# Reordering the delta-rule stage of a two-block layer: convolution taps in halves, squares, norms and the last pair's gate at other places of the queues

## The reference, cut to what matters

```python
def _gdn_mixer(h, w_in, conv_w, a_log, dt_bias, o_gain, w_out):
    ...
    proj = h @ w_in
    qkv = jax.nn.silu(_causal_conv(proj[..., :3 * W], conv_w)).astype(jnp.float32)
    z = proj[..., 3 * W:4 * W]
    ...
    q = _l2norm(qkv[..., :W]) * (Dh ** -0.5)
    k = _l2norm(qkv[..., W:2 * W])
    beta = jax.nn.sigmoid(b_raw)
    g = -jnp.exp(a_log) * jax.nn.softplus(a_raw + dt_bias)
    o = _chunk_gated_delta(q, k, v, g, beta)
    o = _rms(o, o_gain) * jax.nn.silu(z)
    return o @ w_out
```

## Time and profile before

| what | value |
|---|---|
| median of 3 runs | 900.2 us (900.01 to 903.18) |
| the profiled execution, its own time | 899.58 us |
| its span, first to last instruction | 897.8 us |
| TensorE / VectorE / ScalarE busy | 811.9 / 639.2 / 497.8 us |
| mean granted TensorE clock | 0.975 |
| stage of the delta rule, in the span | about 478 to 709 us |

### The profile page before, as it was taken

How to read it: one execution, slowest core, us unless ns; L and a number is a source line. 1 busy time by engine, 2 the same in 40 slices (tenths; PEclk the granted TensorE clock), 3 DMA queues, 4 the chain that set the end, 5 groups by cost and what they waited for, 6 DMA issues and landing times.

```text
span 897.8 us, 16865 instructions
## 1 busy us (share of the span) xinstructions
PE 811.9 (90%) x7056; PEld 752.0 (84%) x7056; DVE 639.2 (71%) x1284; ACT 497.8 (55%) x1013; POOL 0.2 (0%) x4
## 2 busy tenths in 40 slices
PE   4988999999999999999978788989888879999988
PEld 3877999989999999999967586868777869978888
DVE  4467977896687888978868677676655577955464
ACT  4566744444556666654555635454662356666862
POOL 0000000000000000000000000000000000000000
PEclk9999999999999999999999899999997999999999
DMA  8522764765455566548762422121224236754211
GB/s 342 208 91 91 260 231 168 281 235 204 172 189 188 206 210 232 201 145 284 267 240 81 153 66 79 58 86 57 87 95 141 95 128 230 284 203 142 94 48 48
DMA packets 22684, 148.50 MB, mean 165 GB/s; under 512 B 2640, under 2 KB 3024, under 8 KB 6480
## 3 DMA queue, kind: packets, MB, share of 16 engines
q1 hardware_dynamic: 22608, 147.43, 46.3%
HBM read 146.37 MB, written 1.05 MB: 164 GB/s over the span
## 4 chain that ended last, share of the span: by engine, by line
PE 66%; DVE 21%; ACT 11%; issue 2%; DMA 1%; SPq 0%; DVEq 0%; ACTq 0%
PE ps L1960 51%; DVE wlo L1467 4%; DVE raw L1488 2%; DVE tmp L1464 1%; DVE qT L1464 1%; DVE vt L1464 1%; DVE kT L1464 1%; ACT L1050 1%; ACT whi L1071 1%; PE pp L2137 1%; PE pp L2114 1%; PE pp L2299 1%; DVE p0lo L1467 1%; PE pp L2178 1%; PE pp L2310 1%
## 5 line engine op out<-in xcount | busy, mean ns | idle before, releaser
L1960 PE MATMUL ps<-p0hi,whi 128*128 128x256 f32 x1128 | 333.0, 295 | 20.8 <-DVE p0lo L1467 13.6
L1960 PE MATMUL ps<-p0lo,whi 128*128 128x256 f32 x1128 | 320.2, 284 | 0.0
L1960 PE MATMUL ps<-p0hi,wlo 128*128 128x256 f32 x1128 | 319.4, 283 | 0.0
L1467 DVE TENSOR_TENSOR wlo<-raw,whi 128x512 fp32r<-128x512 f32 (+2 forms) x436 | 274.3, 660 | 22.3 <-ACT whi L1071 21.9
L1960 PEld LDWEIGHTS ps<-p0hi,whi 128*128 128x128 f32 x1128 | 217.1, 192 | 33.5 <-issue 15.7
L1071 ACT ACTIVATE whi<-raw 128x512 fp32r<-128x512 f32 (+2 forms) x436 | 238.6, 599 | 2.7 <-DMA raw<-wst 2.7
L1960 PEld LDWEIGHTS ps<-p0lo,whi 128*128 128x128 f32 x1128 | 217.4, 193 | 0.9 <-issue 0.7
L1960 PEld LDWEIGHTS ps<-p0hi,wlo 128*128 128x128 f32 x1128 | 217.1, 192 | 0.0
L1488 DVE CUSTOM_DVE_ANT_0 raw<-raw,cact,vc 128x1024 f32<-128x1024 f32 x64 | 81.8, 1278 | 0.0
L1960 PE MATMUL ps<-zhi,whi 128*128 128x256 f32 x176 | 49.8, 283 | 0.9 <-DVE wlo L1467 0.9
L1960 PE MATMUL ps<-zlo,whi 128*128 128x256 f32 x176 | 49.1, 279 | 0.0
(11 more groups left out here) (344 smaller groups left out, 1357.8 us busy)
## 6 DMA issues: line engine op xcount, KB each, us to landing
raw<-wst SPq DMA_DIRECT2D x125, 1024.0 KB, 4.9
raw<-wsd SPq DMA_DIRECT2D x16, 704.0 KB, 4.0
x<-xT SPq DMA_DIRECT2D x4, 256.0 KB, 5.1
m_x<-memT SPq DMA_DIRECT2D x1, 1024.0 KB, 8.6
outT<-x SPq DMA_DIRECT2D x4, 256.0 KB, 2.4
cact<-cB SPq DMA_DIRECT2D x1, 512.0 KB, 13.7
cst<-con SPq DMA_DIRECT2D x1, 356.0 KB, 12.0
smo<-conr SPq DMA_DIRECT2D x1, 320.0 KB, 11.7
```

What stands on the lines that cost most here:

```text
L1467: return v.tensor_tensor(lo, src, hi.bitcast(F32), ALU.subtract)
L1960: ins = t.matmul(o, a, b, start=first and q == 0, stop=last and q == len(ops) - 1, skip_group_check=True)
```

## The change

In the list: the taps of a unit are put off in two halves, one to each of the next two steps (half 0, one tile, then half 1, the other tile), and the SiLUs go with the second. The gate's transpose `g_tp` goes one round behind its copy `g_cp`; `g_ctp` and `g_col` come one round sooner, `g_exp` and `g_c3` stay in their round. `d_ones` comes one round behind `d_sq`, where two stood between, and `d_nrm`, `d_vtp`, `d_vb` one round behind `d_rs`. `d_on` comes a round behind `d_ors`. For pair 3 alone, `d_oz` reads the PSUM bank and multiplies by gain and gate, and `d_on` then multiplies by the norm; `d_ohi` and `d_olo` follow at a round's distance each. In the engines' code, only the taps' loop, `d_on`, `d_oz` and the names waited for differ; the number of instructions is the same.

```diff
 def on_mqk(i):
     def rest():
-        add("ctap", i)
+        add("ctap", i, 1)
         ...
-    later(rest)
+    self.deferred.extend([lambda: add("ctap", i, 0), rest])
 def on_qkva(u):
     def rest():
-        add("gtap", u)
+        add("gtap", u, 1)
         if u >= 8:
             add("gsilu", u - 8)
-    later(rest)
+    self.deferred.extend([lambda: add("gtap", u, 0), rest])
 def gdn_gates():
     ...
     add("g_cp", 2)
+    yield
     add("g_tp", 2)
-    yield
     add("g_abs", 2)
     ...
     add("g_m", 2)
-    for _ in range(4):
+    for _ in range(3):
         yield
     add("g_ctp", 2)
     add("g_col", 2)
+    yield
     add("g_exp")
     add("g_c3")
 def gdn(i):
     ...
     yield
-    yield
     for n in range(2):
         add("d_ones", i, n)
         add("d_rs", i, n)
+    yield
+    for n in range(2):
         add("d_nrm", i, n)
     ...
     add("d_oones", i)
     add("d_ors", i)
+    if i == 3:
+        add("d_oz", i)
+        add("d_on", i)
+        yield
+        add("d_ohi", i)
+        yield
+        add("d_olo", i)
+        return
+    yield
     add("d_on", i)
 def frees(name, i):
+    if name in ("mqk", "qkva"):
+        return on(FREES[name], i, 1)
 # VectorE, d_on
+    if n_ == 3:
+        e.wait_ge(*on("d_oz", n_))
+        v.tensor_tensor(qv, qv, tr[3 * (n_ % 2)], ALU.mult).then_inc(*tick("d_on"))
 # VectorE, d_oz
+    if n_ == 3:
+        e.wait_ge(*on("d_osq", n_))
+        stt(qv, ps[3 + 2 * (n_ % 2)], V("o_gain"), zv, ALU.mult, ALU.mult).then_inc(*tick("d_oz"))
```

More of the change, by code:

```diff
@@ L1156, in _ @@
                     v = flat(mqk[:, 2 * n:2 * n + 2, :])
-                    e.wait_ge(*on("ctap", n))
+                    e.wait_ge(*on("ctap", n, 1))
                     silu(v, v).then_inc(*tick("csilu"))
@@ L1221, in _ @@
                     n, = i
-                    e.wait_ge(*on("gtap", n + 8))
+                    e.wait_ge(*on("gtap", n + 8, 1))
                     for v in (qT, kT):
@@ L1416, in _ @@
                     n_, = i
-                    e.wait_ge(*on("d_oz", n_))
+                    e.wait_ge(*on("d_on" if n_ == 3 else "d_oz", n_))
                     e.wait_ge(*unit_done("za", 3))
@@ L1578, in _ @@
                 elif kind in ("ctap", "gtap"):
-                    n, = i
+                    n, m = i
                     if kind == "ctap":
@@ L1586, in _ @@
                         e.wait_ge(*on("gid", n))
-                    for m in range(2):
-                        for s in range(1, 4):
-                            if s > 1:
-                                e.wait_ge(*own.last)
-                            o = dst[:, m * T + s:(m + 1) * T]
-                            ins = stt(o, bank[:, m * T:(m + 1) * T - s], V(wname, (2 * n + m) * 4 + 3 - s), o, ALU.mult, ALU.add)
-                            if m * s == 3:
-                                ins.then_inc(*tick(kind))
-                            else:
-                                own.mark(ins)
+                    for s in range(1, 4):
+                        if s > 1:
+                            e.wait_ge(*own.last)
+                        o = dst[:, m * T + s:(m + 1) * T]
+                        ins = stt(o, bank[:, m * T:(m + 1) * T - s], V(wname, (2 * n + m) * 4 + 3 - s), o, ALU.mult, ALU.add)
+                        if s == 3:
+                            ins.then_inc(*tick(kind))
+                        else:
+                            own.mark(ins)
                 elif kind == "mv":
@@ L1884, in _ @@
                     n_, = i
+                    qv = flat(qT[:, 2 * n_:2 * n_ + 2, :])
                     e.wait_ge(*on("d_ors", n_))
-                    stt(flat(qT[:, 2 * n_:2 * n_ + 2, :]), ps[3 + 2 * (n_ % 2)], V("o_gain"), tr[3 * (n_ % 2)], ALU.mult, ALU.mult).then_inc(*tick("d_on"))
+                    if n_ == 3:
+                        e.wait_ge(*on("d_oz", n_))
+                        v.tensor_tensor(qv, qv, tr[3 * (n_ % 2)], ALU.mult).then_inc(*tick("d_on"))
+                    else:
+                        stt(qv, ps[3 + 2 * (n_ % 2)], V("o_gain"), tr[3 * (n_ % 2)], ALU.mult, ALU.mult).then_inc(*tick("d_on"))
                 elif kind == "d_oz":
@@ L1889, in _ @@
                     qv = flat(qT[:, 2 * n_:2 * n_ + 2, :])
-                    e.wait_ge(*on("d_on", n_))
+                    zv = flat(sz[:, 2 * n_:2 * n_ + 2, :])
                     e.wait_ge(*on("za", n_))
-                    v.tensor_tensor(qv, qv, flat(sz[:, 2 * n_:2 * n_ + 2, :]), ALU.mult).then_inc(*tick("d_oz"))
+                    if n_ == 3:
+                        e.wait_ge(*on("d_osq", n_))
+                        stt(qv, ps[3 + 2 * (n_ % 2)], V("o_gain"), zv, ALU.mult, ALU.mult).then_inc(*tick("d_oz"))
+                    else:
+                        e.wait_ge(*on("d_on", n_))
+                        v.tensor_tensor(qv, qv, zv, ALU.mult).then_inc(*tick("d_oz"))
                 elif kind == "d_olo":
```

## The result

The changed kernel took 887.1 us (median of 4 runs, 884.65 to 890.77) against 900.2 us (4 runs, 900.01 to 903.18): a ratio of 0.985, 95% interval 0.981 to 0.989. The forecast was 886.0 with a range of 881 to 894. The profiled execution took 884.65 us, the fastest of the four and 2.5 under their median.

What follows compares the result with a forecast made beforehand. In the stage no engine is full; engines wait for each other, TensorE standing still 33.7 us. Terms 5.4 + 1.4 + 5.1 - 0.95 + 3.4 + 1.0 - 1.2 - 1.4 = 12.7, plus 1.3 clock: 886 us, range 881 to 894.

Steps and rivals of the forecast that it cites:

- Norms behind their roots: d_vtp's wait on TensorE for ScalarE's Ln and Exp, four times up to 1.5 us: all 5.1 us go.
- Taps in halves: Halved VectorE taps free TensorE's d_uu (5.4 us, four places) and d_v1 (1.4 us, two places): all gone.
- What it costs: three rounds: Pairs run later, d_olo of pair 3 in round 76 instead of 73; costs 1.2 us at outa's opening, 1.4 in the tail.
- Squares: Squares one round ahead of d_ones: new waits of 0.6 us at pair 1, 0.35 at pair 2; 0.95 charged, ends 0 and 3.9.
- Output norm: d_on a round behind d_ors: TensorE's d_x wait for d_u, 3.4 us in three places, 2.6 at pair 2, all goes.
- Gates: Ahead of the first squares only VectorE's gain counts, as g_abs starts sooner: 1.0 us, ends 0 and 2.9.
- Opening, 5.4, and tail: Waits where outa opens (rounds 64 to 67) sum to 5.4 us, so +1.2; pair 3's chain after d_o 5.1 us, so +1.4.
- Clock: Half-clock stretches at 642.5 and 673.3 us recover, one more comes at the opening or tail: net 1.3 us back, ends ±3.4.
- ScalarE's two loads: za 0's SiLU before pair 3's Ln saves a pair of table loads, 2 x 1.28 us on ScalarE, nothing on the path.
- move to the squares: Rival, chance 0.20: d_ones waits for the squares as d_vtp did for the roots; 5.1 us return, 892.6 us median.
- the waits were not TensorE's to give: Rival, chance 0.04: behind each wait that goes the next stands, leaving the time within 0.5% of 900.2 us.
- The low clock from the opening of outa on: Rival, chance 0.04: rounds 64 to 76 and the residual parts mostly at half clock, some 25 us more, 912.5 us median.

Runs made afterwards that it cites:

- e11: The changed kernel run again with no edit, as the measure for the others: 888.2 us, ratio 0.988.
- e3: Changed kernel with d_nrm, d_vtp and d_vb back in the round of d_rs, an empty round behind: 900.3 us, ratio 1.002.
- e9: Kernel before with squares one round ahead of d_ones and norms one round behind the roots, no pair later: 898.1 us, ratio 0.998.
- e10: Kernel before with norms a round behind the roots, squares left two rounds ahead, each pair a round longer: 902.4 us, ratio 1.004.
- e1: Changed kernel with both tap halves in the first of the two steps, SiLUs and rounds unchanged: 887.3 us, ratio 0.987.
- e12: Kernel before, taps whole, with only the SiLUs one step later, so pairs run a round later against the taps: 898.7 us, ratio 0.999.
- e2: Changed kernel with d_on of pairs 0 to 2 back in the round of d_ors, an empty round behind: 890.3 us, ratio 0.991.
- e4: Changed kernel with g_tp back in the round of its copy g_cp: 885.0 us, ratio 0.985.
- e8: Changed kernel with pairs 0 to 2 parked at their sums and, once za is through, parked pairs called ahead of active ones: 879.7 us, ratio 0.978.
- e6: Changed kernel with the squares two rounds ahead of d_ones again: 888.5 us, ratio 0.988.
- e7: Changed kernel with pair 3's d_on and d_oz in the old order and form, all rounds kept: 889.1 us, ratio 0.989.
- e5: Changed kernel with pairs 0 to 2 parked as soon as their sums are issued, so pairs 2 and 3 begin a round sooner: 883.5 us, ratio 0.983.

## Why the prediction was right, and where it was not

*The sum.* 12.7 us of waiting were forecast to go and 1.3 us of clock. Measured: the stage's standing still fell from 33.7 to 21.0, by 12.7 us, and its busy time by 2.2. The sum is closer than its terms, as the next points show, and so in part luck. In the medians 13.1 us went (10.5 in the group of e11), against the 14 forecast.

*Norms behind their roots, 5.1.* Right in size: the wait is gone, and e3 brings 5.2 back. But the step "5.1 go" had the price of TensorE's own wait only. Undone, it costs about 13 us in the median, because VectorE's queue bunches up behind the norms (the two further waits of e3, 3.7 us less the 0.2 that the changed kernel has) and because the clock is lower too (0.967 against 0.973 in the median of the runs). And the term does not stand alone: on the kernel before, the same move gives nothing or less (e9, e10).

*Taps in halves, 5.4 and 1.4.* The waits went as forecast, for a cause other than the one named. The step that failed is "in halves a round carries 1.47 us of taps, and every one of the four waits is shorter than the 1.47 put off". e1 keeps the six taps together and loses neither wait nor, in the median, time; e12 leaves everything else as before, shifts the pairs by one round, and 5.4 becomes 0.5. Two of the four waits were 1.7 us and so longer than 1.47; the prediction covered them by "or stands behind d_on as well", and they went by the shift too. The shift stood in the prediction as a cost only ("What it costs: three rounds"), when it was also what moved the taps out from in front of d_xm.

*Squares, 0.95.* 0.72 at pair 1 against 0.6; at pair 2 no wait for squares, but 0.22 at d_uu against 0.35. The first wait, pair 0's 3.9, stayed at 4.0.

*Output norm, 3.4.* The waits went; the 0.8 that is left at d_x is the first wait of the opening, forecast as 0.75. By e2 the part itself holds 1.4 us, less than half of what the step gave it, and by e12 the shift alone takes 1.5 of the 2.6 at pair 2.

*Gates, 1.0.* Forecast between 0 and 2.9. "Only what VectorE gains counts" was the right step: its standing still behind g_abs fell from 3.09 to 1.36 us, and from g_mm to the first sums of squares, with the same rounds between them, the changed kernel takes 27.36 us where the kernel before takes 28.87, 1.5 less. Only 0.4 of that shows as less waiting, 2.93, 0.43 and 3.91 before, 0.45, 0.84, 1.57 and 4.00 after; in the kernel before the rest was busy time, at a clock of 0.92 against 1.00. The half taps are part of it (e1, 28.17), g_tp's round is not (e4, 27.34).

*Opening, 5.4, and tail.* Worked out as 0.75, 1.15, 2.3, 1.2; measured 0.79, 1.24, 2.45, 1.34, in sum 5.8, which makes the term 1.6 instead of 1.2. The wait for `p0lo` was to be about 8 and is 8.6. The chain was to be 5.1 us and is 5.3. The 6.6 us of the stretch before are 6.5 by its own rows. In the tail TensorE waits 0.69 and 3.55 us where it waited 2.94, so 1.3 more against the 1.4 forecast. That 0.69 of it now shows as a wait of d_oones was not named apart. Those places were priced by laying the queues side by side, and that is why they fit.

*Clock, 1.3.* At 642 us the clock is full (1.00), as forecast. At 673 it is not: outa opens there now, and 671.6 to 674.9 has 0.53. Two more stretches at half are at 548.6 and 592.9, with TensorE busy through both. Net it came out at about 2.5 us of busy time less in one execution, 0.7 in the other (811.2). The bounds of 3.4 us to both sides held it, but the runs do not bear out a clock given back: over ten runs the changed kernel's clock is 0.967 to 0.981, median 0.973, and that of the kernel before is no lower (median 0.977 over 49). The profiled execution, the fastest of its four, had the highest of the ten.

*ScalarE's two loads.* 22 instead of 24, and nothing on the path. In the trace the Ln starts 0.01 us after its load ends:

```profile
582.97 1.28 ACT L1063 ACT_TABLE_LOAD   x1
584.26 0.69 ACT L1380 ACTIVATE tr<-pp,cst 128x512 f32<-128x512 f32 x1
```

The Trainium skill (ScalarE: Activation LUTs, What ACT_TABLE_LOAD costs) counts a drain of about 1.4 us beside the load; by the trace a switch costs the 1.28 of the load here, and the measurement decides.

*The rivals.* The wait did not move to the squares in the changed kernel, but in e9 it does, at 1.1 us in each of three pairs: it was the right rival, held off by the step that the SiLUs and the pairs moved. e12 ends at the time of "the waits were not TensorE's to give", but by another way: 5 us of waiting did go, and the clock took them back. The low clock from the opening of outa on did not decide the result, but a part of it is there: in e11 667.4 to 681.0 is at 0.50 throughout, 13.6 us, where the kernel before has 6.8 at that place and 3.4 ahead of it.

What stays open: why the clock of some orders is lower than that of others with as much waiting. It is not the luck of one profile: e3, e10 and e12 have medians of 0.967, 0.967 and 0.969 over ten runs each, e9 and the kernel before 0.975 and 0.977, and e8 0.981 in every run. For e2, e6 and e7, with four runs each, the ranges overlap with the changed kernel's, and nothing is told.

## What to carry to other kernels

In a list of jobs shared by in-order engines, a change of one round has two effects: it covers the wait that it was made for, and it shifts everything behind it against what stays in place, here the taps. Price both, and test a part both by taking it out of the new order and by putting it alone into the old one; the norms were worth 13 us by the first and nothing by the second. Where the consumer of the stage waits for one small job, put that job ahead of the others in its engine's queue: in e8 that took the waits for `p0lo` in the opening from 5.0 us (e5) to 0.8. And read the clock of every run, not of the profiled one alone, before a saving in waiting is counted as time.

## What the runs showed of the hardware

The same kernel, with the same waits, ran one profiled execution with TensorE busy for 809.4 us at a mean clock of 0.981 and another for 811.2 at 0.969. Between orders the difference is larger: the 7056 matmuls took from 807.9 us (e8, clock 0.981) to 820.4 us (e3, clock 0.964). In e3 7.9 us more of standing still than in e11 came with 9.2 us more of busy time; by the medians, 12 us more, a microsecond of stall cost there about one and a half. In e12 5.1 us less of it than before came with 5.5 us more of busy time.

Total idle time alone does not set the clock: e9 and e10 stand still for the same 86.4 us, and their clocks are 0.968 to 0.983 and 0.964 to 0.970 over ten runs each, their busy times 810.0 and 815.7 us. The Trainium skill (TensorE: Matmul & The Clock Gate, HAM oscillation — how this bites in real kernels) warns of idle gaps between bursts. Which gaps matter no run here shows: the lowest clocks are those of e3, which has many waits of 1 to 2 us in the middle of the stage, of e2 (0.965 in its profile), which has hardly more than the changed kernel, and of e10, which has two of about 5.
